# Stick-breaking attention in layer 1: the weights become the stationary operand, each head's values are computed by themselves, and the work around them is moved

## The reference

```
def stick_breaking_attention(q, k, v):           # q, k, v: (1, 528, 16, 64)
    z = einsum('bqhd,bkhd->bhqk', q, k) * scale  # for blocks of queries, keys up to the block's end
    log_1m = where(strict, log_sigmoid(-z), 0)
    after = cumsum(log_1m, reverse=True) - log_1m
    w = where(strict, exp(log_sigmoid(z) + after), 0)
    out = einsum('bhqk,bkhd->bqhd', w, v)
```

## Time and profile before

| | |
|---|---|
| median of 3 runs | 1887.18 us (1886.69 to 1887.96) |
| the profiled execution's own time | 1886.69 us |
| its span, first to last instruction | 1884.7 us |
| PE / DVE / ACT / POOL busy | 97% / 65% / 40% / 4% of the span |
| mean granted TensorE clock | 0.994 of full speed |

### The profile page before, as it was taken

One profiled execution on the slowest core, in us unless ns is written; L12 is line 12 of the kernel. 1 busy time (PEld: TensorE's weight loads), 2 busy tenths in 40 slices (PEclk: granted clock), 3 DMA queues, 4 the chain that ended last, 5 costly groups with the idle time before them and its releaser, 6 DMA issues.

```text
span 1884.7 us, 36044 instructions
## 1 busy us (share of the span) xinstructions
PE 1825.9 (97%) x14286; PEld 1737.0 (92%) x14286; DVE 1221.8 (65%) x1740; ACT 755.5 (40%) x1135; POOL 68.5 (4%) x140
## 2 busy tenths in 40 slices
PE   7999999999999999999999999999899999999996
PEld 7999998999899999999998888888789999999996
DVE  7787756455456777774334777777775688878323
ACT  5444432121234222222224777777774422223221
POOL 0122220000000000000000000000000000000000
PEclk9999999999999999999999999999999999999998
DMA  4222213222222222232222111111112222223221
GB/s 150 91 80 79 90 49 111 68 68 67 68 71 86 89 89 89 89 97 95 90 78 72 58 59 49 59 58 59 57 45 79 89 89 89 89 89 102 93 92 60
DMA packets 39938, 149.92 MB, mean 80 GB/s; under 512 B 4384, under 2 KB 5408, under 8 KB 39216
## 3 DMA queue, kind: packets, MB, share of 16 engines
q1 hardware_dynamic: 38672, 142.16, 24.1%
q10 hardware_dynamic: 1184, 6.60, 1.0%
HBM read 146.62 MB, written 2.13 MB: 79 GB/s over the span
## 4 chain that ended last, share of the span: by engine, by line
PE 71%; issue 12%; DVE 9%; ACT 6%; POOL 2%; DMA 0%; DVEq 0%; ACTq 0%; POOLq 0%
PE gp L359 60%; PE small L403 3%; PE small L414 3%; DVE spb L1502 1%; DVE sp_lo L1524 1%; ACT lbuf L922 1%; DVE wlo L1059 1%; ACT lbuf L925 1%; PE small L576 1%; POOL dec L1664 1%; PE small L553 1%; ACT whi L661 1%; PE small L561 1%; ACT L927 1%; ACT L995 0%
## 5 line engine op out<-in xcount | busy, mean ns | idle before, releaser
L359 PE MATMUL gp<-hn_hi,whi 128*128 128x264 f32 x3216 | 664.6, 288 | 23.0 <-DVE wlo L1059 12.2
L359 PE MATMUL gp<-hn_hi,wlo 128*128 128x264 f32 x3216 | 657.4, 286 | 0.0
L359 PE MATMUL gp<-hn_lo,whi 128*128 128x264 f32 x3216 | 656.7, 286 | 0.0
L661 ACT ACTIVATE whi<-raw 128x1024 fp32r<-128x1024 f32 (+1 forms) x249 | 273.6, 1099 | 775.5 <-PE gp L359 774.5
L1059 DVE TENSOR_TENSOR wlo<-raw,whi 128x1024 fp32r<-128x1024 f32 (+1 forms) x249 | 317.5, 1275 | 390.1 <-ACT whi L661 389.6
L359 PEld LDWEIGHTS gp<-hn_hi,whi 128*128 128x128 f32 x3216 | 503.0, 189 | 29.2 <-DVE wlo L1059 14.2
L359 PEld LDWEIGHTS gp<-hn_hi,wlo 128*128 128x128 f32 x3216 | 500.7, 189 | 0.0
L359 PEld LDWEIGHTS gp<-hn_lo,whi 128*128 128x128 f32 x3216 | 500.3, 189 | 0.0
L359 PE MATMUL gp<-hid_hi,whi 128*128 128x264 f32 x704 | 142.6, 284 | 0.0
L359 PE MATMUL gp<-hid_lo,whi 128*128 128x264 f32 x704 | 142.5, 284 | 0.0
L359 PE MATMUL gp<-hid_hi,wlo 128*128 128x264 f32 x704 | 142.5, 283 | 0.0
(11 more groups left out here) (241 smaller groups left out, 1907.1 us busy)
## 6 DMA issues: line engine op xcount, KB each, us to landing
raw<-in SPq DMA_DIRECT2D x217, 512.0 KB, 3.6
raw<-in SPq DMA_DIRECT2D x32, 704.0 KB, 4.1
cs_bc<-cs_scratch ACTq DMA_DIRECT2D x4, 1056.0 KB, 6.2
hT<-in SPq DMA_DIRECT2D x4, 528.0 KB, 7.4
out<-yT SPq DMA_DIRECT2D x4, 512.0 KB, 2.8
rdec<-in ACTq DMA_DIRECT2D x1, 1056.0 KB, 8.9
gw<-in SPq DMA_DIRECT2D x8, 128.0 KB, 3.4
rope<-in ACTq DMA_DIRECT2D x1, 528.0 KB, 5.8
```

The costliest lines, as they stand in the source:

```text
L359: ins = pe.matmul(gp[t.par][:, h, 0:H2], wp[w.par][:, cols], rp[:, k0 + k, h * H2:(h + 1) * H2], start=first and k == 0 and n == 0, stop=l ...
L661: act.activation(whi[w.par][:, 0:kt * P], raw[w.par][:, 0:kt * P], ACT.Copy).then_inc(hi_done, 1)
```

## The change

- The values of a head are computed by `mix_values`: 15 blocks of weights per head, each stationary once while 64 columns of values stream. The result is token-major in bank 3 (320 columns of a head). `values(n, e)` is called for each head.
- DVE's new `take_head(n, e)` copies it to the new tile `so_tok`; PE's new `heads_out(n)` transposes `so_tok` back to channel-major (5 transposes), and ACT's `l1_heads_out` copies that into `yT`, the last 16 columns after the next block's `gates`.
- On PE `values(n, 0)` stands behind `scores(n, b, 1)` (unit 3, k = 4), `suffix(n, 1)` behind the last step of unit 4, `values(n, 1)` behind k = 3 of the next unit 0, and `heads_out(n)` before `gates(n+1)`. `ysb_done` is waited for in `v_out` in place of `gates`.
- On ACT `weigh(n-1, 1)` comes before `y_part` in the last block, `lru_root` before `l1_heads_out`, and `split(5)` behind `soft(n, 1)` in place of inside it.
- On DVE `take_head(n-1, 1)` comes before `lru_out`, `take_head(n, 0)` before `soft(n, 1)`, and `tile(3)` and `split(5)` in this order behind `soft(n, 1)` in place of before it.

```diff
-            def values(n):
-                pe.wait_ge(w_done, 2 * n + 2)
-                for e in range(2):
-                    c = slice(HEAD * e, HEAD * (e + 1))
-                    pe.matmul(sp_[c, 1, 32:32 + N_META], sv_tok[:, 0, c], wts[e][:, 0:N_META], start=True, stop=True)
-                for j in range(NT):
-                    q0 = max(N_META, P * j)
-                    for e in range(2):
-                        c = slice(HEAD * e, HEAD * (e + 1))
-                        ins = pe.matmul(sp_[c, 3, q0 - N_META:512], sv_tok[0:SZ[j], j, c],
-                                        wts[e][0:SZ[j], OFF[j] + q0 - P * j:OFF[j] + WJ[j]], start=j == 0,
-                                        stop=j == NT - 1, skip_group_check=True)
-                ins.then_inc(pv_done, 1)
+            def values(n, e):
+                pe.wait_ge(w_done, 2 * n + e + 1)
+                wait_count(pe, so_done, 2 * n + e)
+                mix_values(wts[e], lambda j: sv_tok[0:SZ[j], j, HEAD * e:HEAD * (e + 1)],
+                           lambda i: sp_[0:SZ[i], 3, HEAD * i:HEAD * (i + 1)], pv_done)
+
+            def heads_out(n):
+                pe.wait_ge(so_done, 2 * n + 2)
+                for i in range(NT):
+                    dst = sp_[:, 3, P * i:P * (i + 1)] if i < 4 else sp_[:, 1, 32:32 + SZ[4]]
+                    ins = pe.transpose(dst, so_tok[0:SZ[i], i, :], ident[0:SZ[i], 0:SZ[i]])
+                ins.then_inc(tso_done, 1)
...
-                if (unit, k) == (0, 2) and before:
-                    suffix(n - 1, 1)
-                if (unit, k) == (0, 5) and before:
-                    values(n - 1)
+                if (unit, k) == (0, 3) and before:
+                    values(n - 1, 1)
                 if (unit, k) == (0, 7):
+                    if before:
+                        heads_out(n - 1)
                     gates(n, b, i)
...
                     scores(n, b, 1)
+                    values(n, 0)
+                if (unit, k) == (4, 7):
+                    suffix(n, 1)
...
+            def l1_heads_out(n, following=True):
+                act.wait_ge(tso_done, n + 1)
+                act.activation(yT[:, n, 0:512], sp_[:, 3, :], ACT.Copy)
+                if following:
+                    act.wait_ge(gates_done, n + 2)
+                act.activation(yT[:, n, 512:T], sp_[:, 1, 32:48], ACT.Copy).then_inc(ysb_done, 1)
...
-                soft(n, 1, lambda: split(5))
+                soft(n, 1, lambda: None)
+                split(5)
...
+            def take_head(n, e):
+                ve.wait_ge(pv_done, 2 * n + e + 1)
+                if e == 0:
+                    wait_count(ve, tso_done, n)
+                c = slice(HEAD * e, HEAD * (e + 1))
+                ve.tensor_copy(so_tok[:, 0:4, c], sp_[:, 3, 0:256].rearrange("p (i d) -> p i d", d=HEAD))
+                ve.tensor_copy(so_tok[0:SZ[4], 4, c], sp_[0:SZ[4], 3, 256:320]).then_inc(so_done, 1)
...
                 gelu_out(n)
+                take_head(n, 0)
+                soft(n, 1)
+                tile(3)
                 split(5)
-                tile(3)
-                soft(n, 1)
```

More of the change, by code:

```diff
@@ L202, in build @@
                 sv_tok = sb("sv_tok", [P, NT, P], f32, s3)
+                so_tok = sb("so_tok", [P, NT, P], f32, s3)
                 lbuf = sb("lbuf", [P, CAUSAL], f32, s3)
@@ L276, in build @@
             sem(n) for n in ("xc_done", "gates_done", "tri_done", "la_done", "lb_done", "root1_done"))
[L277 to L280, removed]
+        z_done, l_done, spf_done, suf_done, w_done, pv_done, so_done = (
+            sem(n) for n in ("z_done", "l_done", "spf_done", "suf_done", "w_done", "pv_done", "so_done"))
+        tvs_done, svtok_done, tso_done, ysb_done, gu_done, gth_done, ylru_done = (
+            sem(n) for n in ("tvs_done", "svtok_done", "tso_done", "ysb_done", "gu_done", "gth_done", "ylru_done"))
         sum_done, sphi_done, later_done, lathi_done, latlo_done = (
@@ L563, in suffix @@
                 ins.then_inc(suf_done, 1)
-            def values(n):
-                pe.wait_ge(w_done, 2 * n + 2)
-                for e in range(2):
-                    c = slice(HEAD * e, HEAD * (e + 1))
-                    pe.matmul(sp_[c, 1, 32:32 + N_META], sv_tok[:, 0, c], wts[e][:, 0:N_META], start=True, stop=True)
-                for j in range(NT):
-                    q0 = max(N_META, P * j)
-                    for e in range(2):
-                        c = slice(HEAD * e, HEAD * (e + 1))
-                        ins = pe.matmul(sp_[c, 3, q0 - N_META:512], sv_tok[0:SZ[j], j, c],
-                                        wts[e][0:SZ[j], OFF[j] + q0 - P * j:OFF[j] + WJ[j]], start=j == 0,
-                                        stop=j == NT - 1, skip_group_check=True)
-                ins.then_inc(pv_done, 1)
+            def values(n, e):
[9 more added lines that the diff above has]
+                ins.then_inc(tso_done, 1)
             def gates(n, b, half_n):
-                wait_count(pe, ysb_done, n)
                 pe.wait_ge(xc_done, n + 1)
@@ L592, in v_out @@
             def v_out(n):
+                wait_count(pe, ysb_done, n)
                 for i in range(4):
@@ L641, in after @@
                 def after(k):
[L642 to L645, removed]
+                    if c == 5 and k == 3:
+                        values(7, 1)
+                    if c == 5 and k == 7:
+                        heads_out(7)
                 hgemm(At(0, 0, W_OUT1 + c), At(0, 0, T_OUT1 + c), after=after)
@@ L830, in _, with y_part @@
                 ret_stage(r)
-            def y_part(dst, tiles, wb, between=None):
+            def y_part(dst, tiles, wb):
                 for k, y in enumerate(tiles):
@@ L837, in y_part @@
                         split_hi(At(0, 0, wb + 1))
-                    if k == 5 and between is not None:
-                        between()
             act.wait_ge(unit_done, W_OUT0)
@@ L945, in weigh @@
                 act.wait_ge(suf_done, 2 * n + e + 1)
-                wait_count(act, pv_done, n)
+                wait_count(act, pv_done, 2 * n + e - 1)
                 for b, w, at in BANKS:
@@ L967, in l1_v @@
                 act.wait_ge(tvs_done, n + 1)
-                wait_count(act, pv_done, n)
+                wait_count(act, pv_done, 2 * n)
                 act.activation(sv_tok[:, 0:4, :], sp_[:, 3, :].rearrange("p (i c) -> p i c", c=P), ACT.Copy)
@@ L1005, in l1_block @@
                 before = not (isinstance(n, int) and n == 0)
+                if before:
+                    weigh(n - 1, 1)
                 if early:
                     act.wait_ge(unit_done, W_OUT1)
-                    y_part(hn_hi, EARLY[1], W_OUT1, lambda: weigh(n - 1, 1))
+                    y_part(hn_hi, EARLY[1], W_OUT1)
                 else:
                     split(1)
-                    if before:
-                        weigh(n - 1, 1)
                 if before:
+                    lru_root(n - 1)
                     l1_heads_out(n - 1)
-                    lru_root(n - 1)
                 l1_gates(n)
@@ L1034, in _ @@
             l1_block(3, 1, early=True)
+            weigh(7, 1)
             split_hi(At(0, 0, W_OUT1 + 6))
-            weigh(7, 1)
-            l1_heads_out(7)
             lru_root(7)
+            l1_heads_out(7, following=False)
             split_hi(At(0, 0, W_OUT1 + 7))
@@ L1607, in l1_block @@
                 if not (isinstance(n, int) and n == 0):
+                    take_head(n - 1, 1)
                     lru_out(n - 1)
@@ L1632, in _ @@
             add_tile(At(0, 0, W_OUT1 + 4), At(0, 0, T_OUT1 + 4), 4)
+            take_head(7, 1)
             split_lo(At(0, 0, W_OUT1 + 6))
```

## The result

The changed kernel takes 1903.62 us (median of 4 runs, 1902.58 to 1904.58), the kernel before beside it 1887.57: a ratio of 1.0083, 95% interval 1.0067 to 1.0097. It is slower, by 16 us (13 to 18 by the interval). The profiled executions lie further apart, 1904.85 against 1886.69.

The account below looks back on a forecast made before the run. PE, busy 97% of the span, bounds the kernel, so its instructions cost in full. 26.4 + 6.0 + 0.7 + 0.6 - 6.1 - 3.5 - 3.1 - 1.5 = +19.5 us on 1886.7 gives 1906, range 1899 to 1915.

Parts of the forecast that it names:

- Values: PE's values in the mixer: the new form adds 3.3 us in each of 8 blocks, 26.4 us, all on PE's path.
- The twin in layer 0: Same function in layer 0, 15 blocks per head, 64 streamed fp32 columns: 6.17 us for two heads, used to price values.
- Heads out: PE's five transposes before the gates: 0.75 us in each of 8 blocks, 6.0 us, in full on PE.
- DVE's copies: `take_head` copying 256 and 64 columns from PSUM: 0.7 us, costing nothing where it ends before PE asks.
- the wait of 0.6 us in the last block: `heads_out` in the last block waits 0.6 us, because DVE casts and convolves before `take_head`.
- The waits that go: PE's waits at `v_out` and in `suffix(n, 1)` disappear: 6.1 us and 3.5 us won.
- What is late next: Next unit 0 waits for DVE's `tile(3)` and `split(5)`: a tie with PE, 0.1 us, 7 times, 0.7 us.
- the tie: At unit 0, `split(5)` ready 13.55 us behind `scores`, PE there at 13.5; up to 1.3 us each if cover is gone.
- The last block: Gap before it falls to 3.2 us, 3.1 won; less half clock, 1.5 won, after 1.0 for the clock falling again.
- Rival 2: DVE bounds each block next: `split(5)` stalls PE 1.0 to 1.3 us in 7 blocks, +8 us, 1914; chance 0.12.
- Rivals 3 and 4: `mix_values` records cheaper than 0.11 us: load hidden, 1888, no change, chance 0.04; or a price between, 1896, chance 0.06.

Follow-up runs that it names:

- b1_root_first: The kernel before with one line moved, ACT's `lru_root` ahead of `l1_heads_out`: 1880.98 us, 0.9972 of the kernel before.
- a5_dve_late: The changed kernel with one more DVE copy between `tile(3)` and `split(5)` in blocks 0 to 6: 1906.17 us, 1.0111 of the kernel before.
- a2_stream32: The changed kernel with 32 in place of 64 columns of values streamed against each standing block: 1925.29 us, 1.0183 of the kernel before.
- a4_casts_first: The changed kernel with `weigh(6, 1)` behind the first four casts of `y_part` in the last block: 1900.97 us, 1.0067 of the kernel before.
- b3_gap_and_first_head: The kernel before, old form, with `lru_root` first, both suffixes and `values` later, `suffix(6, 1)` in the gap before the last block: 1866.71 us, 0.9885.
- c1_new_form_old_order: The new form (`mix_values`, `take_head`, transposes) in the old order, with `lru_root` first: 1922.17 us, 1.0182 of the kernel before.

## Why the prediction was right

The forecast was 1906, range 1899 to 1915; measured 1903.6.

- *Values.* The step that carries the sum, 26.4 us, measured 26.6. The twin in layer 0 gave 6.17 us for two heads; here they take 3.13 + 3.03. The twin's price held in another place, and its large records are 0.112 us apart in both.
- *Heads out.* 6.0 against 6.4, shown by taking four transposes away.
- *DVE's copies.* 0.42 and 0.20 us, 0.47 from the first's start to the next work's, against 0.7. They were covered, as was said, and the wait of 0.6 us in the last block didn't come.
- *The waits that go.* `v_out` 6.1 against 6.5; b1_root_first shows that moving the root ahead of the heads is enough. `suffix(n, 1)` was under-sized: its floor is 2.23 us, not 2.4, and so each call won 0.75 and not 0.5. That is 1.8 us over 7 calls and the largest error of the sum.
- *What is late next.* A tie, as forecast. DVE's and PE's timelines of the changed kernel at one start of a unit 0:

```profile
1111.37 1.21 DVE L1061 TENSOR_TENSOR wlo<-raw,whi 128x1024 fp32r<-128x1024 f32 x1
...
1112.61 0.34 PE L562 MATMUL small<-wlo,neg_r 128*128 128x384 f32 x1
1112.79 0.44 PE L360 MATMUL gp<-hn_hi,whi 128*128 128x264 f32 x2
```

  `wlo` is done at 1112.58, PE starts at 1112.79. I put 0.7 us on the tie and it cost none; a5_dve_late shows what it costs once it is lost.
- *The last block.* The gap of 3.2 us was 3.1. The clock fell, to which I had given 0.6. It fell for half as long as before, but the call of `suffix` that used to run in the slow stretch now runs ahead of it, and the loss is split otherwise between the rows of the ledger than in the sum (-1.5 forecast, 0 measured). The recorded working has a slip of 0.1 us here: 13.5 + 1.42 + 0.15 is 15.1, not 15.2. Whether the clock falls isn't settled by the length of the idle time alone: it fell in five of the six traces with 2.9 to 3.3 us of idle time at this place (not in a2_stream32's), not in a4_casts_first's with 1.1 us, and again in b3_gap_and_first_head's with waits of 0.95 us and less. So no run shows that a shorter gap keeps the clock full.

Rival 2 (DVE the next bound) didn't come about; it was 0.2 us away. Rivals 3 and 4, cheaper records, are refuted by the records themselves: 0.112 us apart in both places. The Trainium skill gives about 81 ns for a pair of weight load and matmul with 128 streamed columns (TensorE: Matmul & The Clock Gate, Back-to-back issue gap). These fp32 records take longer, although they stream 64. The Trainium skill's advice where the right-hand side has at most 64 columns is to swap the operands and tile the columns (TensorEngine Tiling (Array Packing), Performance Considerations). The runs agree: the form it describes is the cheaper one here, by the 33 us of c1_new_form_old_order.

The forecast difference was +19.5 us. The ledger has +17.3, the profiled executions +18.2, the medians +16.0 with an interval of 13 to 18. So the ledger accounts for 2.2 us of the miss, and what is left is within the scatter. That the sum came this close is in part luck: the errors at `suffix(n, 1)` (2.8) and at the tie and the last block's wait (1.3) went one way, the clock (1.5) the other.

## What to carry to other kernels

Where an engine is busy for 97% of the time, price a rewrite by its start-to-start cost on that engine, from a twin elsewhere in the same trace, and only then add what a better order wins. Test order and form apart: here the form cost 33 us, the order gave some 17 back, and that and more (21.7 us) was to be had with the old form by moving a few calls on ACT and PE. A wait for a chain on other engines is often cured by arriving one step later with other work in between, but work taken away from that place brings the wait back. Before a fall of the clock is put down to an idle time, look for the same idle time in the other traces.

## What the hardware did that I hadn't expected

- The granted clock can fall with no idle time just before it. With 32 streamed columns per standing block it fell to half behind the scores in every block, with 48 in three of eight, with 64 in none. With half the columns streamed the kernel was about 20 us slower (19 by the ratios, 22 by the medians).
- The same idle time doesn't always bring the half clock. Between 991 and 996 us PE idles for 2.4 to 2.5 us in each of the twelve traces: in seven of them, the kernel before's too, the clock then falls to half for 3.4 us, in five, the changed kernel's too, it stays full:

```profile
992.90:995.70 2.80, 0.43 (x4) 0.21 (x2) 2.14 (x4) 2.19 (x3) 0.00 (x0) 1.00 0.00 0
995.80:999.20 3.40, 3.40 (x28) 3.40 (x29) 1.80 (x2) 0.00 (x0) 0.00 (x0) 1.00 0.65 169
```

  These are the changed kernel's stretches, beside the first two of the earlier trace rows. Of the longer idle times before the last block, those of 6.1 us came with 6.8 us at half clock in all four traces.
- In a record with 128 standing columns the streamed ones were free, up to 64: 0.112 us whether 32, 48 or 64 streamed. With 16 standing they set the time: 0.029, 0.043 and 0.056 us.
- PE stood for 5 us at the second turn of its loop, with nothing to wait for, in one kernel of the twelve traced.
